# The last 11 taps of a 31-tap convolution on GpSimd instead of VectorE, in a two-block model kernel

## The chip, the cores and the metric

The kernel runs on one core of a Trainium2 chip. The metric is the device time of one execution in microseconds, as the median of several runs. The engines of the core that matter here are TensorE (matrix products; PE in the rows), VectorE (DVE), ScalarE (ACT) and GpSimd (POOL). Each works off its own queue in order and waits on semaphores for the others. SBUF is the memory on the chip that all of them read and write; products go to PSUM, which TensorE writes.

## What is computed

Two stacks of two layers over 256 tokens of width 1024. The change is in the mixer of the second stack, `hybrid_mixer`, which runs once in each of its two layers. It projects the normalised rows to several parts and feeds three branches: a gated linear attention (mLSTM, 4 heads), a gated convolution over 256 channels with 31 taps, and a softmax attention with decay (8 heads). Cut to the convolution:

```python
CONF_CHANNELS = D_MODEL // 4     # 256
CONF_KERNEL = 31

def causal_dwconv(x, w, b):
    K, C = w.shape
    y = lax.conv_general_dilated(
        x, w.astype(jnp.float32)[:, None, :], window_strides=(1,), padding=[(K - 1, 0)],
        dimension_numbers=("NWC", "WIO", "NWC"), feature_group_count=C)
    return y + b.astype(jnp.float32)

def hybrid_mixer(h, w_in, ...):
    z = jnp.einsum("bsd,de->bse", h, w_in).astype(jnp.float32)
    ...
    a, g = jnp.split(c_glu, 2, axis=-1)
    hc = causal_dwconv(a * jax.nn.sigmoid(g), conf_conv_w, conf_conv_b)
    hc = jax.nn.silu(layernorm_f32(hc, conf_ln_w, conf_ln_b))
    ...
    cat = jnp.concatenate([hm, hc, hf], axis=-1).astype(h.dtype)
    return jnp.einsum("bse,ed->bsd", cat, w_out)
```

So each of 256 channels is a sum over 31 shifts of its own row of 256 tokens, each times a number of that channel.

## The kernel before

The 256 channels lie as 2 halves of 128 partitions. `cf_in` holds the gated input, 2 x (30 + 256) columns with 30 zero columns ahead; `cf` is the accumulator, 128 x 2 x 256; `cw` and `cb` are weights and bias. `convolve` (line 2741) issues one VectorE instruction for each tap and half: for tap 0 a product with bias (line 2748, one input), for the others a product added to the accumulator (line 2749, both inputs in SBUF), 128x256 each. Each waits for the instruction two places ahead of it, which wrote the same half. `gate_glu` (line 2758) forms the gated input from two projection results, with one VectorE product of 128x512 (line 2760).

The list `glu` (line 2775) cuts this into nine steps: `glu[0]` the gate, `glu[1]` to `glu[7]` four taps each, `glu[8]` three. `hybrid_mixer` builds a list of jobs for `projection` (line 627), and puts `glu[0]` to `glu[4]` (16 taps) between the last projections. A job is one product on TensorE of a 128x2048 weight tile (48 matmuls of 128x256, since each product is made of three, line 129 to 131, over a high and a low part). The high part is rounded by ScalarE (line 112), the low part is what VectorE subtracts from it (line 116, 128x2048, both inputs in SBUF; called a split below). VectorE meets in its queue, from the gate on: taps 0 to 3, a split, taps 4 to 7, a split, taps 8 to 11, a split, taps 12 to 15. The three splits belong to the last three jobs (two give `h_fk`, the third `h_fv`). ScalarE takes their results (lines 2659, 2660), and between the last two it computes the exponentials of the decay and a sigmoid-weighted product (lines 2770 to 2773).

A join of all four engines ends the projection. Then come two calls of `attention` (line 674): first the softmax attention with 8 heads, 4 units of work, then the gated one with 4 heads, 2 units. VectorE's part is a loop over x: `prepare(x)` scales scores, `finish(x - 3)` normalises the output of a unit into `cat`, and `between[x]` runs what was handed in. Before, the first call runs `glu[5]` at x = 2 and `glu[6]` at x = 3, the second `glu[7]` at x = 2 and `glu[8]` at x = 3. At x = 1 of the second, VectorE also splits the first two weight tiles of the output projection. A join ends each call. `hybrid_tail` then transposes `cf` and `cat` on TensorE, normalises the convolution's channels and writes them to `cat[:, :, 256:512]`, whose columns nobody wrote before.

GpSimd in all this issues a few parameter transfers and three memsets, one of which clears the zero columns of `cf_in`, and then waits in the joins.

Of the kernel before, what the change touches and what calls it, by code (L numbers as in the profile page):

```python
# [12 lines left out]
ALU = mybir.AluOpType  # L13
# [3 lines left out]
P = 128  # L17
TOK = 256
# [2557 lines left out]
ML_H, ML_D, FX_H, FX_D = 4, 64, 8, 64  # L2576
ML_W, CF_W, FX_W = ML_H * ML_D, D // 4, FX_H * FX_D
ML_K, CF_K = 4, 31
# [69 lines left out]
def hybrid_mixer(c, layer, cat, buffers, claims, ahead):  # L2648

    nc, arg = c.nc, c.arg  # L2650
# [4 lines left out]
    def decay(buf, n, t):  # L2655
        return buf[:, 0:n * P].rearrange("p (h k) -> p h k", h=n) if t == 0 else \
            buf[:, n * P:].rearrange("p (h k) -> p h k", h=n)
# [5 lines left out]
    padded = c.sig("conv_padded")  # L2663
# [5 lines left out]
    step, convolved = c.sig("conv_step"), c.sig("convolved")  # L2669
# [71 lines left out]
    def convolve(dve, taps, n, x, acc, wt, b):  # L2741

        for k in taps:
            for i in range(n):
                if k:
                    dve.wait_ge(step.sem, step.count - n + 1)
                src = x[:, i, k:k + TOK]
                last = nc.vector.tensor_scalar(acc[:, i, :], src, wt[:, i, 0:1], b[:, i:i + 1], ALU.mult, ALU.add) if k == 0 else \
                    nc.vector.scalar_tensor_tensor(acc[:, i, :], src, wt[:, i, k:k + 1], acc[:, i, :], ALU.mult, ALU.add)  # L2749
                last.then_inc(*step.up())  # L2750

    def convolve_qk(dve):
# [2 lines left out]
        convolve(dve, range(ML_K), NT, qk_in, qk, mw, mb)  # L2755
        dve.drain().then_inc(*convolved.up())

    def gate_glu(dve):
        dve.wait_ge(*taken_act.at(4))
        c.dve(nc.vector.tensor_tensor(cf_in[:, :, cpad:], cf_in[:, :, cpad:], sg[:, :, :], ALU.mult))  # L2760

    def taps_glu(k0, k1):
        return lambda dve: convolve(dve, range(k0, k1), 2, cf_in, cf, cw, cb)

    def decay_exps(act):
# [6 lines left out]
        act.wait_ge(*convolved.at(1))  # L2772
        nc.scalar.activation(qk[:, :, :], qk[:, :, :], ACT.Silu)

    glu = [Step("dve", gate_glu)] + [Step("dve", taps_glu(k, min(k + 4, CF_K))) for k in range(0, CF_K, 4)]
    more = [
        Rows(c.xs, w, Z_V, HV, "act", cp(vo[:, :, 0:HV])),
        Cols(c.xs, w, Z_FQ, 256, "act", scaled_copy(fq[:, 0:2, :])),
# [22 lines left out]
    @c.block.gpsimd  # L2801
    def _(pool):
        pool.wait_ge(*c.sig("rms_turned").now())
# [4 lines left out]
    def _(pool):  # L2808
# [2 lines left out]
        nc.gpsimd.memset(fv[:, :, FX_W:], 0.0)  # L2811
        pool.drain().then_inc(*padded.up())
    projection(c, jobs, join=False)
    c.join()
    half = lambda i: slice((i % 2) * 64, (i % 2) * 64 + 64)
    third = c.xT[:, 0:2, :].rearrange("p k t -> p (k t)")
    attention(c, [(t, 0) for t in range(TT)], FX_H, FX_D,
# [1 line left out]
              v=lambda b, i, s: fv[:, s, i * FX_D:i * FX_D + P],  # L2819
              out=lambda t, b: cat[:, t, ML_W + CF_W:].rearrange("p (h d) -> p h d", h=FX_H),  # L2820
              scale=1.0, bias=lambda t, h, nk: decay(df, FX_H, t)[:, 4 * h:4 * h + 4],
              between={2: glu[5].run, 3: glu[6].run}, third=third)
    og = vo[:, :, ML_W:]

    @c.block.scalar
    def _(act):
# [2 lines left out]
              q=lambda t, b, i: qk[half(i), i // 2, t * P:(t + 1) * P], k=lambda b, i, nk: qk[half(i), 2 + i // 2, 0:nk],  # L2829
              v=lambda b, i, s: vo[:, s, i * ML_D:i * ML_D + P],  # L2830
              out=lambda t, b: cat[:, t, 0:ML_W].rearrange("p (h d) -> p h d", h=ML_H),
              scale=ML_D ** -0.5, bias=None, between={2: glu[7].run, 3: glu[8].run}, third=third,
              gated=(lambda t, nk: decay(dm, ML_H, t), lambda t: floor[:, t, :]))
    hybrid_tail(c, cat, cf, vo, norm_w, ln_w, ln_b)

# [290 lines left out]
def build(nc, arg, out):  # L3126
    with ExitStack() as ctx:
# [7 lines left out]
        def stages():  # L3135
# [21 lines left out]
            for layer in range(DEPTH):  # L3157
                with ExitStack() as m:
                    cat = c.sb(f"cat{2 + layer}", [P, TT, D], ctx=m)
                    gain = c.gain[:, :]  # L3160
                    if layer == 0:
                        gain = cat[:, 0, :]
                        load_ahead(c, "gain_landed", [(gain, bcast(arg["norm_mix_w_2"][0]))])
                        post_norm(c, columns=False)
                    hybrid_params = hybrid_buffers(c, layer, m)
                    pre_norm(c, gain)
                    jobs = residual_jobs(c, c.xs, arg["w_out_2"][layer], 1.0)
                    hybrid_mixer(c, layer, cat, hybrid_params, claims, lambda: claim(c, jobs))
                dense = []

                def claim_dense():
                    start, tiles = claim_dense_ffn(c)
                    dense.append(start)
                    return tiles
                cross_attention(c, layer, jobs, claim_dense if layer == 0 else None)
                if layer == 0:
                    claims = dense_ffn(c, dense[0])
                else:
                    flat_moe(c, layer)
# [42 lines left out]
```

## Time and profile before

| | us |
|---|---|
| median of 3 runs | 2651.18 |
| lowest and highest | 2651.12, 2653.88 |
| the profiled execution, time | 2649.35 |
| the profiled execution, span of the trace | 2647.6 |
| its mean granted TensorE clock, share of full speed | 0.939 |

Busy in the span: TensorE 2300.4 us (87%), VectorE 1798.0 (68%), ScalarE 1368.1 (52%), GpSimd 67.5 (3%). Times in the rows count from the start of the span. The 1.75 us that the profiled execution's time lies above its span stand around it and are not in the trace. A row's duration includes some overlap with the next: instructions of one engine that follow each other start a little before the one ahead ends.

### The profile page before, as it was taken

The page shows a single profiled execution, that of the slowest core. Times are in us where ns is not written, and L with a number is a line of the kernel's source. Part 1 is how long each engine was busy: PE and PEld are TensorE (multiplying, and loading weights), DVE is VectorE, ACT ScalarE, POOL GpSimd, SP SyncE. Part 2 cuts the span into 40 slices and gives each one's busy share as a digit, 9 for nine tenths or more (in the row PEclk, how much of TensorE's full clock was granted, in tenths as well). Part 3 has the DMA queues.
Part 4 walks back from the last instruction along what each step waited for, and adds up shares of the span by engine and source line. Part 5 has one row for each costly group of instructions (what it writes and reads, how often), then busy time and mean ns, then how long its engine had stood idle before and what let it go on. Part 6 is the DMA issues. An engine that isn't in the chain of part 4 may idle for free.

```text
span 2647.6 us, 43661 instructions
## 1 busy us (share of the span) xinstructions
PE 2300.4 (87%) x16404; PEld 2139.5 (81%) x16404; DVE 1798.0 (68%) x2101; ACT 1368.1 (52%) x1563; POOL 67.5 (3%) x111
## 2 busy tenths in 40 slices
PE   5568999788769999786889987777999999999997
PEld 4458999776569999775789877667999999998996
DVE  3457777434576765677456657646888888888886
ACT  3316556224345554444343344434777777777775
POOL 0010000000000000100000010000000000000000
PEclk8879999887889999898999999898999999999999
DMA  6227999460239998532345562333999999999993
GB/s 219 80 82 283 373 372 359 137 191 1 83 114 364 364 358 319 142 112 80 127 144 191 159 166 98 96 127 106 312 364 345 345 365 343 344 364 344 339 366 135
DMA packets 335529, 609.66 MB, mean 230 GB/s; under 512 B 11008, under 2 KB 266832, under 8 KB 310704
## 3 DMA queue, kind: packets, MB, share of 16 engines
q1 hardware_dynamic: 329696, 590.84, 63.9%
q0 software_dynamic: 5024, 13.16, 2.2%
q8 instruction: 185, 3.03, 0.5%
q10 hardware_dynamic: 560, 2.10, 0.2%
q14 instruction: 64, 0.52, 0.1%
HBM read 605.02 MB, written 1.05 MB: 229 GB/s over the span
## 4 chain that ended last, share of the span: by engine, by line
PE 77%; DVE 12%; ACT 4%; issue 3%; DVEq 2%; POOLq 1%; DMA 0%; ACTq 0%; POOL 0%; PEldq 0%
PE psum L129 16%; PE psum L131 16%; PE psum L130 16%; PE psum L1887 9%; PE psum L1923 9%; PE psum L1911 2%; DVE weight_ring_rounded L116 1%; PE psum L487 1%; DVE h_cf L2749 1%; ACT scores L760 1%; PE psum L2233 1%; PE psum L712 1%; PE psum L2420 1%; PE psum L548 1%; PE psum L309 1%
## 5 line engine op out<-in xcount | busy, mean ns | idle before, releaser
L1652 DVE TENSOR_TENSOR weight_ring_rounded<-weight_ring,weights_high_rounded 128x2048 fp32r<-128x2048 f32 x264 | 604.1, 2291 | 94.1 <-ACT weights_high_rounded L1647 93.9
L1647 ACT ACTIVATE weights_high_rounded<-weight_ring 128x2048 fp32r<-128x2048 f32 x264 | 504.7, 1915 | 105.4 <-PE psum L131 97.2
L129 PE MATMUL psum<-weights_high_rounded,scores_rounded 128*128 128x256 f32 x1408 | 406.2, 288 | 11.4 <-DVE scores_rounded L1684 10.5
L131 PE MATMUL psum<-weights_high_rounded,scores_rounded 128*128 128x256 f32 x1408 | 398.7, 283 | 0.0
L130 PE MATMUL psum<-weight_ring_rounded,scores_rounded 128*128 128x256 f32 x1408 | 398.4, 283 | 0.0
L1981 DVE TENSOR_TENSOR weight_ring_rounded<-weight_ring,weights_high_rounded 128x2048 fp32r<-128x2048 f32 x128 | 292.7, 2291 | 95.7 <-ACT weights_high_rounded L1976 95.7
L129 PEld LDWEIGHTS psum<-weights_high_rounded,scores_rounded 128*128 128x128 f32 x1408 | 270.0, 192 | 16.3 <-DVE scores_rounded L1684 12.1
L1887 PE MATMUL psum<-weights_high_rounded,scores_rounded 128*128 128x256 f32 x1024 | 263.7, 295 | 12.4 <-DVE scores_rounded L2060 10.7
L130 PEld LDWEIGHTS psum<-weight_ring_rounded,scores_rounded 128*128 128x128 f32 x1408 | 270.2, 192 | 3.4
L131 PEld LDWEIGHTS psum<-weights_high_rounded,scores_rounded 128*128 128x128 f32 x1408 | 270.0, 192 | 0.0
L131 PE MATMUL psum<-weights_high_rounded,xT_rounded 128*128 128x512 f32 (+3 forms) x688 | 261.5, 380 | 0.0
L1923 PE MATMUL psum<-xT_high,weight_ring 128*128 128x128 f32 x2048 | 241.6, 276 | 16.7 <-issue 12.3
L1887 PE MATMUL psum<-weight_ring_rounded,scores_rounded 128*128 128x256 f32 x1024 | 253.1, 285 | 0.0
L1923 PEld LDWEIGHTS psum<-xT_high,weight_ring 128*128 128x128 f32 x2048 | 234.6, 192 | 20.5 <-issue 15.8
L1976 ACT ACTIVATE weights_high_rounded<-weight_ring 128x2048 fp32r<-128x2048 f32 x128 | 243.7, 1905 | 3.2 <-POOLq L212 3.0
L129 PE MATMUL psum<-xT_high_rounded,weights_high_rounded 128*128 128x256 f32 x768 | 217.0, 283 | 14.8 <-DVE weight_ring_rounded L116 9.8
L116 DVE TENSOR_TENSOR weight_ring_rounded<-weight_ring,weights_high_rounded 128x2048 fp32r<-128x2048 f32 (+3 forms) x76 | 159.8, 2113 | 95.9 <-ACT weights_high_rounded L112 95.6
L131 PE MATMUL psum<-xT_high_rounded,weight_ring_rounded 128*128 128x256 f32 x768 | 215.5, 281 | 0.0
L1887 PEld LDWEIGHTS psum<-weights_high_rounded,scores_rounded 128*128 128x128 f32 x1024 | 197.7, 193 | 13.1 <-DVE scores_rounded L2060 10.9
L1887 PEld LDWEIGHTS psum<-weight_ring_rounded,scores_rounded 128*128 128x128 f32 x1024 | 198.2, 194 | 0.4 <-issue 0.4
L112 ACT ACTIVATE weights_high_rounded<-weight_ring 128x2048 fp32r<-128x2048 f32 (+3 forms) x76 | 133.8, 1768 | 117.4 <-PE psum L131 62.9
L130 PE MATMUL psum<-xT_rounded,weights_high_rounded 128*128 128x256 f32 x672 | 188.5, 281 | 0.0
(525 smaller groups left out, 4075.0 us busy)
## 6 DMA issues: line engine op xcount, KB each, us to landing
weight_ring<-in_moe_w_gate_dram SPq DMA_DIRECT2D x152, 1024.0 KB, 6.4
weight_ring<-in_moe_w_up_dram SPq DMA_DIRECT2D x152, 1024.0 KB, 8.4
weight_ring<-in_moe_w_down_dram SPq DMA_DIRECT2D x152, 1024.0 KB, 8.5
weight_ring<-in_w_in_dram SPq DMA_DIRECT2D x20, 1024.0 KB, 7.0
weight_ring<-in_ffn_w_gate_dram SPq DMA_DIRECT2D x11, 1024.0 KB, 5.4
weight_ring<-in_ffn_w_up_dram SPq DMA_DIRECT2D x11, 1024.0 KB, 5.3
weight_ring<-in_ffn_w_down_dram SPq DMA_DIRECT2D x11, 1024.0 KB, 4.9
weight_ring<-in_w_out_dram SPq DMA_DIRECT2D x8, 1024.0 KB, 5.0
```

What stands on the lines that cost most here:

```text
L112: self.ring.nc.scalar.activation(self.high, self.whole, ACT.Copy).then_inc(self.ring.high_ready, 1)
L116: self.ring.nc.vector.tensor_tensor(self.low, self.whole, self.high.bitcast(F32), ALU.subtract).then_inc(self.ring.split_ready, 1)
L129: nc.tensor.matmul(out, lh, rh, start=start, stop=False)
L130: nc.tensor.matmul(out, lh, rl, start=False, stop=False)
L131: return nc.tensor.matmul(out, ll, rh, start=False, stop=stop)
L1647: self.c.nc.scalar.activation(ring.high(self.s0 + q, 1, SLOT), ring.view(self.p0 + q, 1, SLOT), ACT.Copy).then_inc(ring.high_ready, 1)
L1652: self.c.nc.vector.tensor_tensor(ring.low(self.p0 + q, 1, SLOT), ring.view(self.p0 + q, 1, SLOT), ring.high(self.s0 + q, 1, SLOT).bitcast( ...
L1887: last = self.c.nc.tensor.matmul(psum[:, x % 2, a * CH:(a + 1) * CH], self.x[:, x % 2, k, :], w[:, k, :], start=(k == 0 and w is high), st ...
L1911: last = nc.tensor.matmul(psum[:, 2 + x % 2, at:at + self.W], blocks[:, a, m, :], self.twice, start=True, stop=True)
L1923: last = nc.tensor.matmul(psum[:, 4 + 2 * (x % 2) + k // 4, (k % 4) * P:(k % 4 + 1) * P], wt[:, m, k * P:(k + 1) * P], self.hidden[:, x % ...
L1976: self.c.nc.scalar.activation(ring.high(s, 1, SLOT), ring.view(self.gate_tile(x) + a, 1, SLOT), ACT.Copy).then_inc(ring.high_ready, 1)
L1981: self.c.nc.vector.tensor_tensor(ring.low(tile, 1, SLOT), ring.view(tile, 1, SLOT), ring.high(s, 1, SLOT).bitcast(F32), ALU.subtract).then ...
```

## The change

Taps 20 to 30 go to GpSimd. After the gate VectorE raises a signal, `gated`. GpSimd, once its three memsets are done, waits for it and then for each of the 11 taps multiplies both halves of the shifted input by the tap's weights, spread over the columns, in one instruction of 128x2x256; the first product goes to `late`, which is `cat[:, :, 256:512]`, each later one to `product`, `cat[:, :, 0:256]`, and is then added to `late` by a second instruction. That is 11 products and 10 sums, and each waits for the one ahead. The join at the end of the projection leaves GpSimd out. `glu` ends with `glu[5]`, which stays at x = 2 of the first attention; at x = 3 of it nothing is left. At x = 2 of the second attention VectorE waits for GpSimd's last signal and adds `late` to `cf`, one instruction of 128x512; at x = 3 nothing is left.

```diff
+    POOL_TAPS = 20
+    late, product = cat[:, :, ML_W:ML_W + CF_W], cat[:, :, 0:CF_W]
+    gated, pool_step, pool_conv = c.sig("glu_gated"), c.sig("pool_conv_step"), c.sig("pool_convolved")
+
     def gate_glu(dve):
         dve.wait_ge(*taken_act.at(4))
         c.dve(nc.vector.tensor_tensor(cf_in[:, :, cpad:], cf_in[:, :, cpad:], sg[:, :, :], ALU.mult))
+        dve.drain().then_inc(*gated.up())
+
+    def add_late(dve):
+        dve.wait_ge(step.sem, step.count)
+        dve.wait_ge(*pool_conv.now())
+        nc.vector.tensor_tensor(cf[:, :, :], cf[:, :, :], late, ALU.add)
...
-    glu = [Step("dve", gate_glu)] + [Step("dve", taps_glu(k, min(k + 4, CF_K))) for k in range(0, CF_K, 4)]
+    glu = [Step("dve", gate_glu)] + [Step("dve", taps_glu(k, min(k + 4, CF_K))) for k in range(0, POOL_TAPS, 4)]
...
     projection(c, jobs, join=False)
-    c.join()
+
+    @c.block.gpsimd
+    def _(pool):
+        pool.wait_ge(*padded.now())
+        pool.wait_ge(*gated.now())
+        for k in range(POOL_TAPS, CF_K):
+            x, w1 = cf_in[:, :, k:k + TOK], cw[:, :, k:k + 1].broadcast_to([P, 2, TOK])
+            if k == POOL_TAPS:
+                nc.gpsimd.tensor_tensor(late, x, w1, ALU.mult).then_inc(*pool_step.up())
+            else:
+                nc.gpsimd.tensor_tensor(product, x, w1, ALU.mult).then_inc(*pool_step.up())
+                pool.wait_ge(*pool_step.now())
+                nc.gpsimd.tensor_tensor(late, late, product, ALU.add).then_inc(*pool_step.up())
+                pool.wait_ge(*pool_step.now())
+        pool.drain().then_inc(*pool_conv.up())
+    c.join(pool=False)
...
-              between={2: glu[5].run, 3: glu[6].run}, third=third)
+              between={2: glu[5].run}, third=third)
...
-              scale=ML_D ** -0.5, bias=None, between={2: glu[7].run, 3: glu[8].run}, third=third,
+              scale=ML_D ** -0.5, bias=None, between={2: add_late}, third=third,
```

VectorE's queue at x = 1 to 3 of the second attention (`L116` the two splits, `L2749` tap steps, `L789` to `L806` the normalisations of the two units):

```order
 L116 TENSOR_TENSOR weight_ring_rounded<-weight_ring,weights_high_rounded 128x2048 [waits scores_scaled,high_parts_ready]
 L116 TENSOR_TENSOR weight_ring_rounded<-weight_ring,weights_high_rounded 128x2048 [waits high_parts_ready]
-L2749 SCALAR_TENSOR_TENSOR h_cf<-h_cf_in,h_cw,h_cf 128x256 [waits conv_step] x8
+L2770 TENSOR_TENSOR h_cf<-h_cf,cat 128x512 [waits pool_convolved,conv_step]
 L789 SCALAR_TENSOR_TENSOR row_sum<-row_sum 128x4 [waits pv_group_done]
 L790 TENSOR_TENSOR row_sum<-row_sum,h_floor 128x4 [waits dve_step]
 L793 RECIPROCAL recip<-row_sum 128x4 [waits dve_step]
 L806 TENSOR_TENSOR cat<-psum,recip 128x256 [waits dve_step]
-L2749 SCALAR_TENSOR_TENSOR h_cf<-h_cf_in,h_cw,h_cf 128x256 [waits conv_step] x6
```

The eight tap steps ahead of the first normalisation became one addition that waits for GpSimd, and the six between the two normalisations went.

GpSimd's queue behind its memsets, in the first of the two layers (the last two rows shown repeat nine times more):

```order
+L2825 UNCONDITIONAL_BRANCH
+L2832 TENSOR_TENSOR cat2<-h0_cf_in,h0_cw 128x2x256 [waits glu_gated,conv_padded]
+L2834 TENSOR_TENSOR cat2<-h0_cf_in,h0_cw 128x2x256
+L2836 TENSOR_TENSOR cat2<-cat2 128x2x256 [waits pool_conv_step]
+L2834 TENSOR_TENSOR cat2<-h0_cf_in,h0_cw 128x2x256 [waits pool_conv_step]
+L2836 TENSOR_TENSOR cat2<-cat2 128x2x256 [waits pool_conv_step]
```

Where GpSimd went on to the join, it now has 21 instructions. VectorE's queue inside the projection, gate, taps 0 to 15 and three splits, is the same before and after, but for the signal behind the gate:

```order
L2760 TENSOR_TENSOR h_cf_in<-h_cf_in,scores 128x2x256 [waits results_taken_act]
L2748 TENSOR_SCALAR h_cf<-h_cf_in,h_cw,h_cb 128x256 [waits dve_step]
L2748 TENSOR_SCALAR h_cf<-h_cf_in,h_cw,h_cb 128x256
L2749 SCALAR_TENSOR_TENSOR h_cf<-h_cf_in,h_cw,h_cf 128x256 [waits conv_step] x6
L116 TENSOR_TENSOR weight_ring_rounded<-weight_ring,weights_high_rounded 128x2048 [waits high_parts_ready]
L2749 SCALAR_TENSOR_TENSOR h_cf<-h_cf_in,h_cw,h_cf 128x256 [waits conv_step] x8
```

These six rows are those of before; a split and eight tap steps follow twice more.

## Rows read from the trace of the kernel before

**Rows 1.** The page: chain that ended last, by engine.
```profile
PE 77%; DVE 12%; ACT 4%; issue 3%; DVEq 2%; POOLq 1%; DMA 0%; ACTq 0%; POOL 0%; PEldq 0%
```

**Rows 2.** Busy time by stretch: end of projection, two attentions, first layer, then second.
```profile
core 0: us, PE busy (x) PEld busy (x) DVE busy (x) ACT busy (x) POOL busy (x), PEclk, DMA share, GB/s
1144.60:1171.00 26.40, 18.92 (x150) 18.56 (x148) 19.21 (x35) 10.72 (x18) 0.00 (x0) 0.94 0.42 132
1171.00:1192.10 21.10, 14.86 (x104) 11.90 (x104) 14.14 (x44) 11.76 (x40) 0.00 (x0) 0.84 0.09 36
1192.10:1208.20 16.10, 6.29 (x53) 5.21 (x53) 14.45 (x34) 7.00 (x8) 0.00 (x0) 0.88 0.00 1
1602.00:1628.40 26.40, 19.11 (x151) 18.74 (x150) 19.19 (x35) 10.75 (x18) 0.00 (x0) 0.94 0.42 132
```

**Rows 3.** Timeline of VectorE, projection: start, duration, instruction, count.
```profile
1143.88 0.69 DVE L2760 TENSOR_TENSOR h_cf_in<-h_cf_in,scores 128x512 f32<-128x512 f32 x1
1144.60 0.73 DVE L2748 TENSOR_SCALAR h_cf<-h_cf_in,h_cw,h_cb 128x256 f32<-128x256 f32 x2
1145.25 2.46 DVE L2749 SCALAR_TENSOR_TENSOR h_cf<-h_cf_in,h_cw,h_cf 128x256 f32<-128x256 f32 x6
1147.63 2.28 DVE L116 TENSOR_TENSOR weight_ring_rounded<-weight_ring,weights_high_rounded 128x2048 fp32r<-128x2048 f32 x1
...
1158.37 2.28 DVE L116 TENSOR_TENSOR weight_ring_rounded<-weight_ring,weights_high_rounded 128x2048 fp32r<-128x2048 f32 x1
1160.57 3.24 DVE L2749 SCALAR_TENSOR_TENSOR h_cf<-h_cf_in,h_cw,h_cf 128x256 f32<-128x256 f32 x8
```

**Rows 4.** Timeline of TensorE: last three jobs, start of attention; idle before in brackets.
```profile
1150.06 0.55 PE L129 MATMUL psum<-xT_high_rounded,weights_high_rounded 128*128 128x256 f32 x1 [4.87 <-DVE weight_ring_rounded L116]
...
1157.13 0.28 PE L129 MATMUL psum<-xT_high_rounded,weights_high_rounded 128*128 128x256 f32 x1
...
1162.78 0.28 PE L129 MATMUL psum<-weights_high_rounded,xT_high_rounded 128*128 128x256 f32 x1
...
1168.12 0.28 PE L131 MATMUL psum<-weights_high_rounded,xT_rounded 128*128 128x256 f32 x1
1171.00 1.16 PE L712 MATMUL psum<-h_fk,h_fq 64*128 64x128 f32 x16 [2.61 <-POOLq L212]
```

**Rows 5.** Timeline of ScalarE, end of projection.
```profile
1170.13 0.58 ACT L2659 ACTIVATE h_fv<-psum 128x512 f32<-128x512 f32 x1
```

**Rows 6.** Chain of waits through both attentions: start, duration, what.
```profile
1185.27 3.16 DVE h_cf L2749 x8
...
1200.45 3.17 DVE h_cf L2749 x8
...
1204.56 2.37 DVE h_cf L2749 x6
```

**Rows 7.** Timeline of TensorE, behind the tap steps of the first attention.
```profile
1189.12 1.13 PE L735 MATMUL psum<-h_fv,probs_turned 128*128 128x128 f32 x8 [0.39 <-DVE cat L806]
```

**Rows 8.** Timeline of GpSimd at two routings, first stack and last layer.
```profile
172.98 2.40 POOL L2174 CAST e_outT<-e_outT 128x512 f32<-128x512 int32 x1
175.33 1.80 POOL L2175 MEMSET e_xg<- 128x2048 f32 x1
...
1795.20 0.55 POOL L2173 IOTA f_outT<- 128x512 int32 x1 [11.19 <-DVEq L206]
1795.82 0.61 POOL L2174 CAST f_outT<-f_outT 128x512 f32<-128x512 int32 x1
```

**Rows 9.** Timeline of VectorE beside them.
```profile
172.62 2.29 DVE L2118 TENSOR_TENSOR weights_high_rounded<-x,weights_high_rounded 128x2048 fp32r<-128x2048 f32 x1 [1.49 <-ACT weights_high_rounded L2113]
...
176.04 1.11 DVE L2511 CAST r_idx_g<-r_firsti 128x2 f32<-128x2 uint32 x1
...
1797.38 2.29 DVE L2118 TENSOR_TENSOR weights_high_rounded<-f_outT,weights_high_rounded 128x2048 fp32r<-128x2048 f32 x1 [1.59 <-ACT weights_high_rounded L2113]
```

**Rows 10.** Groups of VectorE by form: busy, mean ns of one.
```profile
L2524 DVE CAST r_idx<-r_topi 128x4 f32<-128x4 uint32 x2 | 0.3, 170 | 0.1
```

## The prediction

> **What bounds the kernel now.** I read the page's chain first, then the busy times by stretch, then the chain of waits through the hybrid mixer, the only place the change touches. Over the whole span TensorE holds 77% of the chain and VectorE 12% [rows 1]. The convolution lies in one of the few stretches where VectorE is the limit. The mixer runs twice, once per layer, with the same pattern 457 us apart [rows 2]. In the stretch from the gated product to the end of the projection VectorE is busy 19.2 of 26.4 us, in the two attentions 14.1 of 21.1 and 14.4 of 16.1 us; GpSimd is empty in all of them.
>
> Inside the projection stretch [rows 3], VectorE runs without a gap from 1144.6 to 1163.8: two first-tap products, 6 tap steps, a weight split, 8 tap steps, a split, 8, a split, 8. A tap step costs 0.41 us by spacing (3.24 us for 8), a split 2.2 to 2.3 us. TensorE has already waited 4.87 us for the first of these splits, takes 7.1 us for the job behind that wait (1150.06 to 1157.13) and 5.65 for the next, of as many matmuls, which it starts without one (to 1162.78). Its first matmul after the wait lasts 0.55 us, the later ones 0.28: the lower and the higher of the clock's two levels, 1.2 and 2.4 GHz. It issues its last matmul at 1168.12 [rows 4]. The third split, ready at 1158.37 + 2.28 = 1160.65, thus has 2.1 us of slack before TensorE needs it. The last result leaves ScalarE at 1170.71, because the exponentials stand ahead of it there [rows 5]; this ends the projection, and attention starts at 1171.0.
>
> In the attentions the chain [rows 6] goes through the tap steps directly: 3.16 us late in the first attention, and 3.17 and 2.37 us in the second.
>
> **What leaves VectorE.** Per layer 22 tap steps go, in groups of 8 (first attention), 8 and 6 (second); the 8 steps of the first attention's earlier place stay. First attention: the 3.16 us stand in the chain, but TensorE had then waited only 0.39 us for the result behind them [rows 7]; next late are the copies on ScalarE. I take 0.4 us. Second attention: VectorE goes from the two weight splits straight through taps and normalisations to the end, so 3.17 + 2.37 = 5.5 us come off in full. One addition of 128x512 is added, priced by the gating product of the same shape, 0.69 us [rows 3]. Gain there 4.8 us, 5.2 us per layer, 10.4 us in all. What is next late there is the tail's own chain, unchanged.
>
> The signal behind the gating product costs a drain that VectorE had in effect paid (it waited for that product anyway): zero. The join that GpSimd no longer takes part in is put down to GpSimd's queue in TensorE's row [rows 4], but GpSimd had nothing to do there; ScalarE came last, at 1170.71, so leaving GpSimd out gives nothing. GpSimd's next transfers (the memory rows and the next parameters) are issued after the later joins, as before; the queue is only moved past by 21 instructions that must be over by the end of the mixer.
>
> **What GpSimd adds.** 21 two-input products and sums per layer, 11 and 10, each 128x512, each waiting for the one before. The trace has no two-input operation on GpSimd. The nearest is a cast of the same shape with one input, 0.61 us, and the next instruction behind a wait on its own signal starts 0.07 us after the end (1795.20 + 0.55 to 1795.82) [rows 8]. Lower bound 0.61 us, if a second operand is free; upper bound 1.8 us, three times that. I take twice the cast, 1.2 us, since two operands are read for each result. The 21 then need 21 x 1.27 = 26.7 us, against about 56 us from 1144.9 until the addition that consumes them is due (some 1200). So by itself the work fits and nobody waits for it.
>
> The Trainium skill (GPSIMD Engine Reference, section Elementwise — side-by-side cycle accounting) gives 4497 ns for a two-input fp32 operation of 2048 elements per partition. Scaled to 512 that is an estimate of 1.12 us, and with it the sum below would end near 2683. No row here shows such an operation.
>
> **What it costs VectorE.** This is the term that decides. The trace shows GpSimd and VectorE shutting each other out. The cast that takes 0.61 us alone took 2.40 us when it started at 172.98, 0.36 us behind a VectorE subtraction with two SBUF inputs: it ended at 175.38, 0.47 us after that instruction had ended at 174.91 [rows 8, 9]. It did not run at part speed beside it, it stood. In the other direction a VectorE cast of 2 elements per partition took 1.11 us, from 176.04 to 177.15, where its sibling takes 0.17 [rows 9, 10]; GpSimd's memset beside it ended at 177.13 [rows 8]. The same subtraction begun at 1797.38 under a GpSimd memset kept its 2.29 us [rows 9], so an operation that only writes does not disturb it. The tap steps, and the splits too, are two-input operations in SBUF like that subtraction, and all 21 GpSimd operations read SBUF.
>
> What no row shows is a two-input VectorE instruction that comes behind a reading GpSimd one. The Trainium skill (SBUF — State Buffer, section Who interferes with whom) says that such a pair contends for a shared read interface and that whoever starts first holds it for the whole instruction, whichever engine that is. The trace agrees in the direction it shows.
>
> I take it that the two alternate: each GpSimd operation, ready 0.07 us after its predecessor, finds a VectorE step of 0.4 us running, waits for its end, then runs for 1.2 us while the next VectorE step stands. Counting two-input VectorE instructions up to and including the third split gives 6 + 1 + 8 + 1 + 8 + 1 = 25, enough to interleave all 21. The first overlaps the one-input first taps by 0.4 us. So the third split ends 21 x 1.2 - 0.4 = 24.8 us later, at 1185.4. TensorE starts its last job 0.2 us later and, coming out of a wait at half clock, needs 7.1 us for it (as from 1150.06 to 1157.13 [rows 4]); the copy takes 0.6. The projection ends at 1193.3 instead of 1170.7, **+22.6 us**. Slack of 2.1 us and the 2.3 us between TensorE's and ScalarE's ends are used up in this; the exponentials on ScalarE, moved along, stay hidden under the last job.
>
> Per layer: +22.6 - 5.2 = +17.4 us; twice +34.8. Against the profiled execution's 2649.35 this is 2684; the median shown is 1.8 us above it (0.07%), so I predict **2685 us**. Nothing returns it later: in both mixers TensorE is idle for the whole delay.
>
> **The rivals.**
> 1. *VectorE keeps the turn, or loses nothing.* If steps issued back to back leave no opening, or such a pair does not collide, GpSimd works only in VectorE's pauses: 8 us before attention (1163.8 to 1171.8) and those of the attentions. From 1145 to 1200.4 that is 55.4 us less 18.8 in the projection, 3.2 of taps and 4.4 of splits, 29 us for 26.7 of work. Cost to VectorE 0 to 2.4 us a layer, so 10.4 us minus at most 4.8: **2641 to 2646**. For it: back-to-back steps overlap in the trace (0.475 us long, 0.41 apart). Against it: the blocked cast of 2 elements shows that GpSimd's hold is respected too.
> 2. *One GpSimd operation for every two VectorE ones.* Then 12 fall before the third split: 14.4 - 0.4 = 14.0 us; TensorE ends at 1181.9, copy 1182.5, +11.8; the other 9 lie in VectorE's pause and cost nothing. 2 x (11.8 - 5.2) = +13: **2664**.
> 3. *The operation is at an end of its bounds.* At 0.61 us the third split is 12.4 us late, +10.2 at the end of the projection, 2 x 5.0: **2661**. At 1.8 us it is 37.4 us late, +35.2, 2 x 30.0: **2711**.
> 4. *GpSimd is late, not VectorE.* If VectorE keeps the turn and an operation takes 1.5 us, 21 of them need 33.0 us of the 29 that VectorE leaves free; the addition, which stands on VectorE ahead of both normalisations of the second attention, waits 4.1 us, and TensorE's tail waits for those. Of the 4.8 + 0.4 us gained 1 is left: no change, **about 2650**. The waiting begins at an operation of 1.3 us; from 1.6 us on it is a loss (at 1.8 us 39.3 us, 10 late, 2661).
>
> **How the numbers follow.** Alternation with an operation of 1.0 to 1.4 us: 50%, 2677 to 2694. Rival 2: 15%. Rival 3: 6% short, 9% long. Rival 1: 13%. Rival 4: 7%. Rival 1 alone is faster by over 0.2% (5.3 us, about what a measurement of this kernel can tell from no change): 0.14 with a little of rival 4. Same 0.07, slower 0.79. The range runs from rival 4 to between 2694 and the long end, **2650 to 2704**, leaving out rival 1 and most of the long case.
>
> **What would show it.** In the trace after: GpSimd operations at 1.2 us alone, longer beside VectorE; tap steps in the projection of about 1.6 us spacing instead of 0.41, splits of 3.4 instead of 2.3; TensorE waiting for the second and third split, where it now waits only for the first; a projection stretch of about 49 us instead of 26.4, and a second attention near 11.3 instead of 16.1. It is wrong if tap steps keep their 0.41 us while GpSimd is busy (rival 1), if they come in pairs between long ones (rival 2), or if the addition is preceded by an idle VectorE (rival 4).

## The result

The changed kernel takes 2678.84 us (median of 4, 2677.98 to 2681.14) against 2652.53 us; the ratio is 1.0095, 95% interval 1.0075 to 1.0115. It is slower, by some 25 us. Predicted was 2685 us, 6 us more; as a change that was 34 us, so the loss was forecast a third too large.

Where it went shows best from three marks in each mixer: the gating product on VectorE, the first score matmul of the first attention, that of the second, and the first transpose of the tail.

| us, first layer / second layer | before | after | difference |
|---|---|---|---|
| gate to first attention | 27.12 / 27.12 | 44.31 / 44.19 | +17.2 / +17.1 |
| first attention | 21.12 / 21.12 | 20.51 / 20.65 | -0.6 / -0.5 |
| second attention | 16.07 / 16.07 | 11.13 / 11.13 | -4.9 / -4.9 |

That is +11.7 us a layer, 23.3 in all, inside the interval of the ratio (19.9 to 30.5 us). The two profiled executions differ by more, 31.8 us of span. 7.5 us of this have arisen before the first mixer's gate (1143.88 before, 1151.42 after), in code that the change leaves alone; in the nine experiments this mark lies between 1147.5 and 1160.2 us, without relation to the edits. So comparisons below count from the gate, and totals are taken from the ratios.

Busy time of the kernel after by the same three stretches (columns as in [rows 2]; the first starts at the end of the gate):

```profile
core 0: us, PE busy (x) PEld busy (x) DVE busy (x) ACT busy (x) POOL busy (x), PEclk, DMA share, GB/s
1152.14:1195.73 43.59, 22.99 (x151) 22.45 (x149) 38.20 (x35) 10.74 (x18) 29.01 (x21) 0.77 0.24 77
1195.73:1216.24 20.51, 14.76 (x104) 11.95 (x104) 11.08 (x36) 11.81 (x40) 0.00 (x0) 0.83 0.11 42
1216.24:1227.37 11.13, 6.28 (x52) 5.19 (x52) 9.52 (x21) 6.97 (x8) 0.00 (x0) 1.00 0.01 1
```

VectorE still has 35 instructions in the first stretch, but they last 38.2 us instead of 19.2. All 21 GpSimd operations lie in it. VectorE's timeline there, which answers [rows 3]:

```profile
1152.27 2.30 DVE L2748 TENSOR_SCALAR h_cf<-h_cf_in,h_cw,h_cb 128x256 f32<-128x256 f32 x2
1154.49 7.89 DVE L2749 SCALAR_TENSOR_TENSOR h_cf<-h_cf_in,h_cw,h_cf 128x256 f32<-128x256 f32 x6
1162.31 3.34 DVE L116 TENSOR_TENSOR weight_ring_rounded<-weight_ring,weights_high_rounded 128x2048 fp32r<-128x2048 f32 x1
1165.57 10.48 DVE L2749 SCALAR_TENSOR_TENSOR h_cf<-h_cf_in,h_cw,h_cf 128x256 f32<-128x256 f32 x8
1175.98 3.13 DVE L116 TENSOR_TENSOR weight_ring_rounded<-weight_ring,weights_high_rounded 128x2048 fp32r<-128x2048 f32 x1
1179.03 6.07 DVE L2749 SCALAR_TENSOR_TENSOR h_cf<-h_cf_in,h_cw,h_cf 128x256 f32<-128x256 f32 x8
1185.02 2.29 DVE L116 TENSOR_TENSOR weight_ring_rounded<-weight_ring,weights_high_rounded 128x2048 fp32r<-128x2048 f32 x1
```

Tap steps stand 1.3 us apart instead of 0.41 (7.89 for 6, 10.48 for 8), until GpSimd is done at 1182.84; the last split takes its old 2.29. GpSimd's timeline beside it:

```profile
1152.33 1.04 POOL L2832 TENSOR_TENSOR cat<-h_cf_in,h_cw 128x512 f32<-128x512 f32 x1 [55.66 <-DVEq L2765]
1153.34 1.08 POOL L2834 TENSOR_TENSOR cat<-h_cf_in,h_cw 128x512 f32<-128x512 f32 x1
...
1162.18 1.32 POOL L2836 TENSOR_TENSOR cat<-cat 128x512 f32<-128x512 f32 x1
1163.58 2.97 POOL L2834 TENSOR_TENSOR cat<-h_cf_in,h_cw 128x512 f32<-128x512 f32 x1
1166.63 1.34 POOL L2836 TENSOR_TENSOR cat<-cat 128x512 f32<-128x512 f32 x1
...
1177.04 3.20 POOL L2836 TENSOR_TENSOR cat<-cat 128x512 f32<-128x512 f32 x1
...
1181.50 1.34 POOL L2836 TENSOR_TENSOR cat<-cat 128x512 f32<-128x512 f32 x1
```

A product takes 1.04 to 1.10 us, a sum 1.26 to 1.36, except for the two that met a split: 2.97 and 3.20. The two engines need not touch the same data for this: the sum at 1162.18 reads and writes `cat`, the split at 1162.31 reads weights and takes 3.34 us instead of 2.28. TensorE's timeline, with what ended its waits, which answers [rows 4]:

```profile
1165.80 0.55 PE L129 MATMUL psum<-xT_high_rounded,weights_high_rounded 128*128 128x256 f32 x1 [13.06 <-DVE weight_ring_rounded L116]
...
1179.25 0.55 PE L129 MATMUL psum<-xT_high_rounded,weights_high_rounded 128*128 128x256 f32 x1 [5.15 <-DVE weight_ring_rounded L116]
...
1195.73 1.05 PE L712 MATMUL psum<-h_fk,h_fq 64*128 64x128 f32 x14 [2.38 <-ACTq L201]
```

It waited 4.87 us for splits in this stretch before, now 18.2 in two waits. The third split, for which the prediction had it wait too, was ready just in time: at 1187.31, and the last job started at 1187.49 without a wait. In the second attention the addition stands where the taps stood and waits for nobody:

```profile
1220.09 4.49 DVE L116 TENSOR_TENSOR weight_ring_rounded<-weight_ring,weights_high_rounded 128x2048 fp32r<-128x2048 f32 x2 [0.29 <-ACT weights_high_rounded L112]
1224.49 0.69 DVE L2770 TENSOR_TENSOR h_cf<-h_cf,cat 128x512 f32<-128x512 f32 x1
```

### The profile page after: what moved, and what is told of

Same layout as the page of the kernel before. It is cut to its first block, busy times and chain, and to the rows that moved or that the text cites. A ratio compares the mean times of both kernels' runs of the same rounds, so it can differ in the third digit from the quotient of the medians.

```text
span 2679.4 us, 43665 instructions
## 1 busy us (share of the span) xinstructions
PE 2310.9 (86%) x16404; PEld 2148.2 (80%) x16404; DVE 1819.4 (68%) x2059; ACT 1369.8 (51%) x1563; POOL 125.8 (5%) x153
## 4 chain that ended last, share of the span: by engine, by line
PE 76%; DVE 12%; ACT 4%; issue 4%; DVEq 2%; POOLq 1%; DMA 0%; ACTq 0%; POOL 0%; PEldq 0%
PE psum L129 15%; PE psum L131 15%; PE psum L130 15%; PE psum L1887 9%; PE psum L1923 9%; PE psum L1911 2%; DVE h_cf L2749 2%; DVE weight_ring_rounded L116 2%; PE psum L487 1%; ACT scores L760 1%; PE psum L2233 1%; PE psum L735 1%; PE psum L712 1%; PE psum L2420 1%; PE psum L309 1%
## 5 line engine op out<-in xcount | busy, mean ns | idle before, releaser
L116 DVE TENSOR_TENSOR weight_ring_rounded<-weight_ring,weights_high_rounded 128x2048 fp32r<-128x2048 f32 (+3 forms) x76 | 163.7, 2164 | 97.3 <-ACT weights_high_rounded L112 96.8
```

Source lines behind the costliest of these rows:

```text
L116: self.ring.nc.vector.tensor_tensor(self.low, self.whole, self.high.bitcast(F32), ALU.subtract).then_inc(self.ring.split_ready, 1)
```

## Is it GpSimd's work, and nothing else of the change?

Theory: VectorE and GpSimd take turns, so that a VectorE instruction stands while a GpSimd operation reads. Rival: the signal, the drain or the join without GpSimd slows the projection. Two kernels take one half of the change each. `left_out`:

```diff
-        nc.vector.tensor_tensor(cf[:, :, :], cf[:, :, :], late, ALU.add)
...
-        for k in range(POOL_TAPS, CF_K):
-            x, w1 = cf_in[:, :, k:k + TOK], cw[:, :, k:k + 1].broadcast_to([P, 2, TOK])
-            if k == POOL_TAPS:
-                nc.gpsimd.tensor_tensor(late, x, w1, ALU.mult).then_inc(*pool_step.up())
-            else:
-                nc.gpsimd.tensor_tensor(product, x, w1, ALU.mult).then_inc(*pool_step.up())
...
-              scale=ML_D ** -0.5, bias=None, between={2: add_late}, third=third,
+              scale=ML_D ** -0.5, bias=None, between={}, third=third,
```

> The changed kernel with GpSimd's 21 operations and the added sum taken out: the last 11 taps are not computed at all; the signal behind the gate and the join without GpSimd stay. Theory of turns (VectorE stands while a GpSimd operation reads): the whole loss lies in GpSimd's operations, so tap steps are back at 0.41 us, the stretch from the gate to attention is 27.1 us as before, and the two attentions are 6.5 us a layer shorter, 5.8 as measured after plus 0.69 for the sum: 2652.5 - 13 = 2639.5, ratio 0.995. Rival, the loss comes from the signal, the drain or the join: the stretch stays near 44 us and the time near 2675.

`both`:

```diff
-        nc.vector.tensor_tensor(cf[:, :, :], cf[:, :, :], late, ALU.add)
+        glu[7].run(dve)
...
-    glu = [Step("dve", gate_glu)] + [Step("dve", taps_glu(k, min(k + 4, CF_K))) for k in range(0, POOL_TAPS, 4)]
+    glu = [Step("dve", gate_glu)] + [Step("dve", taps_glu(k, min(k + 4, CF_K))) for k in range(0, CF_K, 4)]
...
-              between={2: glu[5].run}, third=third)
+              between={2: glu[5].run, 3: glu[6].run}, third=third)
...
-              scale=ML_D ** -0.5, bias=None, between={2: add_late}, third=third,
+              scale=ML_D ** -0.5, bias=None, between={2: add_late, 3: glu[8].run}, third=third,
```

> GpSimd's 21 operations of the changed kernel beside all 31 taps on VectorE as before; GpSimd's sum is computed and thrown away, and no tap is missing. Theory of turns: the stretch from the gate to attention is 44.3 us as in the changed kernel (27.1 before), the attentions as before, 2652.5 + 2 x 17.2 = 2687, ratio 1.013. Rival, the two engines do not disturb each other and the change loses by its order or a wait: ratio 1.000.

| | ratio to before | gate to first attention | first attention | second |
|---|---|---|---|---|
| left_out | 0.9951 (0.9934 to 0.9968) | 27.4 / 27.2 | 20.5 / 20.6 | 10.5 / 10.5 |
| both | 1.0125 (1.0100 to 1.0150) | 44.2 / 44.1 | 21.1 / 21.1 | 16.1 / 16.1 |
| after | 1.0095 (1.0075 to 1.0115) | 44.3 / 44.2 | 20.5 / 20.7 | 11.1 / 11.1 |

The two halves fit together without a rest: the whole loss of the stretch comes with GpSimd's operations, the whole gain with the taps taken from VectorE, and signal and join cost 0.1 to 0.3 us (27.4 and 27.2 against 27.12). The rival is out. First stretch of `both`:

```profile
1155.25:1198.75 43.50, 22.73 (x150) 22.16 (x149) 38.20 (x35) 10.72 (x18) 29.02 (x21) 0.76 0.25 80
```

## What of GpSimd collides: reading, writing, or being busy?

`memsets` puts in the place of each operation a memset of about its length, which reads nothing; the last 11 taps are thus left out. It was run once:

```diff
-                nc.gpsimd.tensor_tensor(product, x, w1, ALU.mult).then_inc(*pool_step.up())
+                nc.gpsimd.memset(cat[:, :, 0:ML_W + CF_W], 0.0).then_inc(*pool_step.up())
```

(and so for the first product and the sums).

> The changed kernel with each of GpSimd's 21 operations replaced by a memset of 1024 elements a partition, about as long (0.95 us from the memset of 960 in the trace), at the same place in its queue and with the same waits; the last 11 taps are not computed, and the zeros are added. Theory that what collides is GpSimd's reading: the tap steps of two inputs go back to 0.41 us and splits to 2.3 while GpSimd is busy, and the stretch from the gate to attention is 27 to 29 us. The two first-tap instructions (one input) took 1.1 us each beside GpSimd's products; if they keep that beside memsets, it is GpSimd's writing that stops them. Rival, any busy GpSimd stops VectorE: tap steps of 1.0 to 1.3 us and a stretch of about 42 us.

VectorE, then GpSimd, in this kernel:

```profile
1148.36 2.17 DVE L2748 TENSOR_SCALAR h_cf<-h_cf_in,h_cw,h_cb 128x256 f32<-128x256 f32 x2
1150.44 2.45 DVE L2749 SCALAR_TENSOR_TENSOR h_cf<-h_cf_in,h_cw,h_cf 128x256 f32<-128x256 f32 x6
1152.81 2.28 DVE L116 TENSOR_TENSOR weight_ring_rounded<-weight_ring,weights_high_rounded 128x2048 fp32r<-128x2048 f32 x1
```

```profile
1150.44 0.98 POOL L2837 MEMSET cat<- 128x1024 f32 x1
1151.47 0.95 POOL L2835 MEMSET cat<- 128x1024 f32 x1
1152.48 0.95 POOL L2837 MEMSET cat<- 128x1024 f32 x1
```

Tap steps (2.45 us for 6) and splits (2.28) have their old times while GpSimd is 94% busy. The two first-tap instructions, of one input, stay at 1.1 us each, where they take 0.73 together otherwise. The stretch is 29.7 and 29.5 us: of its 2.4 to 2.6 us more, 1.5 are these two instructions and the signal: the first split is ready that much later. The rest is TensorE's clock: after the longer wait 24 and 22 of its matmuls stand 0.21 us apart (the lower level) instead of 13, and each of these costs 0.1 us more than one at the higher level. So a two-input VectorE instruction collides with a GpSimd operation that reads and not with one that only writes, and a one-input TENSOR_SCALAR with both. Why the second kind collides the traces suggest: in the kernel before, 128x1024 of it take 0.744 us (line 3004) and 128x256 take 0.410, 0.43 ns an element, where a two-input instruction of 128x2048 and one of 128x512 differ by 1.04 ns an element (2.28 and 0.69 us). By these times it moves about two elements where the other moves one. The Trainium skill (VectorE: DVE Perf Modes, section Mode 2×_2P — use both read ports for one tensor) says that such single-input instructions use both read and both write ports; the memset run agrees.

## Turns, or the time that GpSimd is busy?

`halves` cuts each operation into two of 128x256, 42 in all:

```diff
-                nc.gpsimd.tensor_tensor(product, x, w1, ALU.mult).then_inc(*pool_step.up())
-                pool.wait_ge(*pool_step.now())
-                nc.gpsimd.tensor_tensor(late, late, product, ALU.add).then_inc(*pool_step.up())
-                pool.wait_ge(*pool_step.now())
+                for i in range(2):
+                    nc.gpsimd.tensor_tensor(product[:, i], x[:, i], w1[:, i], ALU.mult).then_inc(*pool_step.up())
+                    pool.wait_ge(*pool_step.now())
+                for i in range(2):
+                    nc.gpsimd.tensor_tensor(late[:, i], late[:, i], product[:, i], ALU.add).then_inc(*pool_step.up())
+                    pool.wait_ge(*pool_step.now())
```

> The changed kernel with each GpSimd operation cut into two of 128x256, 42 in all; nothing else differs. Theory of strict turns: one GpSimd operation fits between two VectorE ones whatever its length, so the tap step beside it falls from 1.3 to about 0.75 us; 27 VectorE instructions up to the third split lose about 0.33 us each, the stretch is near 36 us instead of 44.3, and GpSimd runs on into VectorE's pause. Rival, VectorE loses the time that GpSimd is busy, however cut: the stretch stays at 44 us or more and tap steps at 1.3 us on average.

VectorE in this kernel:

```profile
1151.82 4.81 DVE L2749 SCALAR_TENSOR_TENSOR h_cf<-h_cf_in,h_cw,h_cf 128x256 f32<-128x256 f32 x6
1156.55 2.81 DVE L116 TENSOR_TENSOR weight_ring_rounded<-weight_ring,weights_high_rounded 128x2048 fp32r<-128x2048 f32 x1
1159.28 6.58 DVE L2749 SCALAR_TENSOR_TENSOR h_cf<-h_cf_in,h_cw,h_cf 128x256 f32<-128x256 f32 x8
```

Tap steps stand 0.81 us apart, and the stretch is 35.1 and 37.7 us instead of 44.3, though GpSimd does the same sums with more overhead and works until 1189, into the first attention. The expectation was 36. The layers differ by the clock: the last job has one matmul at TensorE's lower level in the first layer and 27 in the second. So VectorE's loss goes by the period of GpSimd's operations, to which each of its short instructions is stretched, and not by GpSimd's busy time. The kernel was run once, in 2660.4 us against 2657.2 for before in the same job; the stretches, with the attentions, ask for 6.6 more. That one time settles nothing, the stretches carry the argument.

`five_taps` leaves only 9 GpSimd operations:

```diff
-    POOL_TAPS = 20
+    POOL_TAPS = 26
...
+    def glu_seven(dve):
+        glu[7].run(dve)
+        add_late(dve)
...
-              between={2: glu[5].run}, third=third)
+              between={2: glu[5].run, 3: glu[6].run}, third=third)
...
-              scale=ML_D ** -0.5, bias=None, between={2: add_late}, third=third,
+              scale=ML_D ** -0.5, bias=None, between={2: glu_seven}, third=third,
```

> The changed kernel with only the last 5 taps on GpSimd (9 operations), the other 26 on VectorE at their former places. Theory of turns: 9 operations stand in front of the first split only; it ends 8 us late, the later two meet a free VectorE, and TensorE, which waits for the first, takes the whole of it: stretch 35 us instead of 27.1. The second attention keeps 4 of 14 tap steps and the sum, 3.2 us shorter. Net +5 a layer: 2656 + 10, ratio 1.004. Rival, the cost is in proportion to the operations (9 of 21): stretch 34.5 us, which is as good as the same; rival, few operations fit into slack: stretch below 30 us and ratio 0.998.

The kernel did not do quite what this says: its last group ran to tap 27, so taps 26 and 27 were added on VectorE too. `five_taps_once` mends that:

```diff
-    glu = [Step("dve", gate_glu)] + [Step("dve", taps_glu(k, min(k + 4, CF_K))) for k in range(0, POOL_TAPS, 4)]
+    glu = [Step("dve", gate_glu)] + [Step("dve", taps_glu(k, min(k + 4, POOL_TAPS))) for k in range(0, POOL_TAPS, 4)]
```

> The last 5 taps on GpSimd (9 operations) and 26 taps on VectorE, each tap once: in the kernel five_taps VectorE also computed taps 26 and 27, 4 tap steps more in the second attention than meant. Theory of turns: the stretch from the gate to attention stays at 35.3 us, the second attention goes from 14.4 to 12.8 us. Net a layer +8.2 - 3.2 = +5, ratio 1.004 with 1.002 to 1.006 allowed. Rival, the 4 steps more were hidden: second attention 14.4 us.

The stretches are 35.3 and 36.0 us with the slip, 36.2 and 36.0 mended; the second attention 14.4 and 12.8 us. Ratios 1.0066 (1.0042 to 1.0089) and 1.0057 (1.0039 to 1.0075), the second near the top of what was allowed. VectorE, mended:

```profile
1155.15 7.90 DVE L2749 SCALAR_TENSOR_TENSOR h_cf<-h_cf_in,h_cw,h_cf 128x256 f32<-128x256 f32 x6
1162.97 3.35 DVE L116 TENSOR_TENSOR weight_ring_rounded<-weight_ring,weights_high_rounded 128x2048 fp32r<-128x2048 f32 x1
1166.24 3.24 DVE L2749 SCALAR_TENSOR_TENSOR h_cf<-h_cf_in,h_cw,h_cf 128x256 f32<-128x256 f32 x8
1169.41 2.28 DVE L116 TENSOR_TENSOR weight_ring_rounded<-weight_ring,weights_high_rounded 128x2048 fp32r<-128x2048 f32 x1
```

All nine are done or under way when the first split starts, the one for which TensorE waits anyway (13.08 us here, 4.87 before), and after them VectorE has its old times. Five taps cost 9 us there: the split comes 8.2 us later, 0.9 for each operation, and the rest is TensorE at its lower level for 10 matmuls more. They bring 3.2 us in the second attention. A few operations at the place without slack cost their full turn.

## Is it the work, or its place?

`late_start` gives GpSimd the same 11 taps but starts it when VectorE is done with the projection:

```diff
+    def free(dve):
+        dve.drain().then_inc(*vector_free.up())
...
-        glu[:2] + more[1:2] + glu[2:3] + more[2:3] + glu[3:4] + more[3:4] + glu[4:5] + more[4:])
+        glu[:2] + more[1:2] + glu[2:3] + more[2:3] + glu[3:4] + more[3:4] + glu[4:5] + more[4:] + [Step("dve", free)])
...
         pool.wait_ge(*gated.now())
+        pool.wait_ge(*vector_free.now())
```

> The changed kernel, but GpSimd waits until VectorE has finished its part of the projection (the 16 taps and three splits). Theory of turns: the stretch from the gate to attention is back at 27.1 us; GpSimd's 21 operations (27 us) run from 1164 on this clock, beside VectorE's pause and the first attention; the 8 tap steps there stand for 0.9 us each, about 7 us a layer, and the end of GpSimd's work at about 1193 is before the sum at about 1198. Net a layer -5.8 + 7 = +1, ratio between 0.998 and 1.003. Rival, the two do not disturb each other: 2652.5 - 11.6 = 2641, ratio 0.9956. Rival, GpSimd then ends too late: VectorE idle before the sum.

The ratio is 1.0029 (1.0019 to 1.0039). The stretch is back at 27.4 us, the first attention takes 29.8 instead of 21.1, the second 11.1. VectorE in the first attention:

```profile
1194.63 0.42 DVE L831 CUSTOM_DVE_ANT_0 scores<-psum,h_df 128x256 f32<-128x256 f32 x1 [3.59 <-PE psum L712]
...
1196.33 10.42 DVE L2749 SCALAR_TENSOR_TENSOR h_cf<-h_cf_in,h_cw,h_cf 128x256 f32<-128x256 f32 x8 [0.23 <-issue]
```

The 8 tap steps take 10.42 us instead of 3.26, 7.2 more, as expected (7). The scaling of scores keeps its 0.42 us with GpSimd busy: one of its inputs comes from PSUM. GpSimd's operations beside such instructions:

```profile
1192.45 1.26 POOL L2841 TENSOR_TENSOR cat<-cat 128x512 f32<-128x512 f32 x1
1193.80 1.04 POOL L2839 TENSOR_TENSOR cat<-h_cf_in,h_cw 128x512 f32<-128x512 f32 x1
1194.92 1.27 POOL L2841 TENSOR_TENSOR cat<-cat 128x512 f32<-128x512 f32 x1
1196.27 1.04 POOL L2839 TENSOR_TENSOR cat<-h_cf_in,h_cw 128x512 f32<-128x512 f32 x1
1197.38 1.33 POOL L2841 TENSOR_TENSOR cat<-cat 128x512 f32<-128x512 f32 x1
```

Both of the engines' times are undisturbed until the tap steps start at 1196.33; then a GpSimd pair goes from 2.47 us (1193.80 to 1196.27) to 2.58, and each tap step loses 0.9. TensorE waits for what comes behind them:

```profile
1209.44 1.11 PE L721 MATMUL psum<-ident,scores 128*128 128x128 f32 x4 [8.98 <-ACT scores L760]
```

The first attention is 9.3 us longer than in the changed kernel, 2.1 more than the tap steps. These 2.1 us lie behind this wait: from there to the second attention it takes 7.88 us (1209.44 to 1217.32), against 5.78 in the changed kernel behind a wait of 1.81, and the granted clock of the attention is 0.71 instead of 0.83. The expectation of 1 us a layer left this out; by the marks it is 4.

If the place decides, the taps need not leave VectorE. `moved` is the kernel before with its last 15 taps at its idle times, 8 us ahead of the first attention and 3.6 us behind its second unit:

```diff
-        glu[:2] + more[1:2] + glu[2:3] + more[2:3] + glu[3:4] + more[3:4] + glu[4:5] + more[4:])
+        glu[:2] + more[1:2] + glu[2:3] + more[2:3] + glu[3:4] + more[3:4] + glu[4:5] + more[4:] + glu[5:7])
...
-              between={2: glu[5].run, 3: glu[6].run}, third=third)
+              between={1: glu[7].run, 3: glu[8].run}, third=third)
...
-              scale=ML_D ** -0.5, bias=None, between={2: glu[7].run, 3: glu[8].run}, third=third,
+              scale=ML_D ** -0.5, bias=None, between={}, third=third,
```

> The kernel before, without GpSimd, with VectorE's last 15 taps at other places: taps 16 to 23 at the end of the projection, where VectorE is idle for 8 us, taps 24 to 27 at x = 1 of the first attention, ahead of an idle time of 3.6 us, taps 28 to 30 at x = 3 of it, none in the second. If what the taps cost is their place and not their number, 2.9 us of the first attention and 5.5 us of the second go, a layer: 2652.5 - 17 = 2635.5, ratio 0.9936. Rival: the pauses are needed (weights, clock) and the time stays.

0.9949 (0.9931 to 0.9968), 2644.43 us against 2656.11 in the same job: faster than both kernels. VectorE:

```profile
1170.51 9.59 DVE L2749 SCALAR_TENSOR_TENSOR h_cf<-h_cf_in,h_cw,h_cf 128x256 f32<-128x256 f32 x24
1181.77 0.69 DVE L840 SCALAR_TENSOR_TENSOR scores<-psum,h_df 128x512 f32<-128x512 f32 x1 [1.68 <-PE psum L712]
...
1184.41 3.25 DVE L2749 SCALAR_TENSOR_TENSOR h_cf<-h_cf_in,h_cw,h_cf 128x256 f32<-128x256 f32 x8
1188.09 0.42 DVE L831 CUSTOM_DVE_ANT_0 scores<-psum,h_df 128x256 f32<-128x256 f32 x1 [0.42 <-PE psum L712]
```

24 tap steps in a row fill the time ahead of the attention and leave 1.68 us of it; 8 more fill the pause behind the second unit and leave 0.42 us. The three stretches are 27.2, 18.6 and 10.5 us, in all 8.0 us less in the first layer (7.1 in the second). The ratio gives 13.5 us (8 to 18), the expectation was 17.

`mixed` is the same idea with GpSimd at a place where nothing collides: taps 16 to 23 on VectorE at the end of the projection, the last 7 on GpSimd from then on, and their addition at the end of the first attention:

```diff
-    POOL_TAPS = 20
+    POOL_TAPS = 24
...
-        glu[:2] + more[1:2] + glu[2:3] + more[2:3] + glu[3:4] + more[3:4] + glu[4:5] + more[4:])
+        glu[:2] + more[1:2] + glu[2:3] + more[2:3] + glu[3:4] + more[3:4] + glu[4:5] + more[4:] + glu[5:7] + [Step("dve", free)])
...
+        pool.wait_ge(*vector_free.now())
...
-              between={2: glu[5].run}, third=third)
+              between={6: add_late}, third=third)
...
-              scale=ML_D ** -0.5, bias=None, between={2: add_late}, third=third,
+              scale=ML_D ** -0.5, bias=None, between={}, third=third,
```

> Taps 16 to 23 on VectorE at the end of the projection, the last 7 taps on GpSimd (13 operations, 16 us), started only then, beside the first attention, in which VectorE now has no tap steps; the sum at its end; no tap step in the second attention. Theory of turns: VectorE's attention instructions read one operand from PSUM and kept their times beside GpSimd before, so nothing collides; the first attention is about 18.5 us (18.6 with the taps moved on VectorE alone), the second 10.5: ratio 0.994 to 0.995, no better than the moved taps without GpSimd. Rival, GpSimd ends after the first attention: VectorE idle before the sum, ratio nearer 0.997.

0.9948 (0.9930 to 0.9966), the same as without GpSimd. Its stretches are 27.3, 19.2 and 10.5 us. GpSimd is done at 1192.15, and the addition stands at 1195.30 for 0.68 us. The first attention is 0.6 us longer than in `moved` in the first layer and as long in the second (19.1). So GpSimd can do this work without harm, but VectorE's idle time was enough for it.

## Why the prediction was right, and where it was off

- **What leaves VectorE.** Predicted 5.2 us a layer, 0.4 in the first attention and 4.8 in the second; measured 0.5 to 0.6 and 4.9. `left_out` has 5.5 in the second, the 5.5 of the two tap groups without the addition.
- **GpSimd's operation.** Taken at 1.2 us between bounds of 0.61 and 1.8. Measured 1.04 to 1.10 for a product, 1.26 to 1.36 for a sum, some 1.2 on the mean; the gap between two is 0.07 to 0.08 us, as read from [rows 8]. The Trainium skill's figure (GPSIMD Engine Reference, section Elementwise — side-by-side cycle accounting), by the estimate 1.12 us, is also near.
- **The turns.** The order was as forecast, one operation for each VectorE instruction: 21 operations fall beside the two first taps and the next two tap groups and splits, and three steps of the third. The size was off. The step that failed is "then runs for 1.2 us while the next VectorE step stands": I added GpSimd's whole 1.2 us to the tap's 0.4, a period of 1.67 us. Measured is 1.29, GpSimd's own period (1.18 for a product, 1.40 for a sum) and hardly more than its 1.24 alone, so most of the tap step must fit into GpSimd's gap and start; it costs GpSimd 0.05 us. VectorE loses 0.9 us a turn, not 1.2. A split of 2.2 us does not fit; there both lose.
- **The first taps.** I took the two one-input instructions to be free of it; they took 2.30 us instead of 0.73. The trace of before could have told, by their time an element. These 1.6 us worked against the turns that were taken too long.
- **The sum.** The third split came 19.1 us late instead of 24.8. And it was not the one that decided: the second, ready 27.7 us behind the gate instead of 11.4, started TensorE's last job but one at 1179.25. That one took 8.2 us, longer than the 7.1 I took for a job behind a wait, since after waits of 13.06 and 5.15 us TensorE stayed at the lower clock level for about 26 matmuls (0.21 us apart until 1184.9; granted clock of the stretch 0.77, before 0.94). In the 7.1 us of before it was some 13, and not only the first one behind the wait, as my reading had it. ScalarE's work behind its result, 7.8 us with the exponentials, then ended the projection: +17.2 us instead of +22.6. In my sum it lay hidden under the last job. Its first and last instruction:

```profile
1187.69 0.60 ACT L2659 ACTIVATE h_fk<-psum 128x512 f32<-128x512 f32 x1 [12.95 <-PE psum L131]
...
1194.86 0.58 ACT L2659 ACTIVATE h_fv<-psum 128x512 f32<-128x512 f32 x1
```

- **The whole.** +11.7 us a layer instead of +17.4, nearly all of the difference in the projection's term. That my path through the third split, with its measured 19.1 us, would have given +16.9, near the +17.2, is luck: the path ran through the second split and ScalarE. Also, 2649.35, 34.8 and 1.8 add up to 2686, not 2685. Rivals 1 and 4 (VectorE keeps the turn) are refuted by the 1.3 us spacing, rival 2 (every other turn) by the one-to-one count, rival 3 by the operation's own time, and nobody waited for GpSimd.

## What to carry to other kernels

Two-input elementwise work given to GpSimd is not beside VectorE if VectorE's own instructions then read two operands from SBUF: here each short one was stretched to GpSimd's period, from 0.41 to 1.3 us. That GpSimd was hardly used before (3% of the span) does not help. What matters is which instructions VectorE runs in that time and whether TensorE waits for them. Those with an operand in PSUM kept their times here (0.42 and 0.69 us in `late_start`), and GpSimd memsets touched only the fast one-input ones. A long wait of TensorE costs more than itself, since it works at the lower clock level behind it: 1.2 us in the changed kernel's last job but one, 2.1 us in `late_start`. Before moving work to another engine, look for the idle times of its own: here 15 taps moved within VectorE's queue gave half a per cent, the same as the best use of GpSimd that was tried.

## What the runs showed of the hardware beyond what was expected

- The turn costs the GpSimd operation almost nothing when the VectorE instruction is short (a pair of operations 2.58 us instead of 2.47 with 0.41 us tap steps between), and VectorE all of it. Beside a 2.2 us split GpSimd's operation takes 2.97 to 3.20 us.
- A one-input fp32 TENSOR_SCALAR between SBUF tensors, 0.32 to 0.37 us a piece, is stopped by GpSimd memsets too (1.1 us a piece); two-input instructions are not.
- A GpSimd sum of two computed tensors takes 1.27 us against 1.04 for a product whose second operand is one number spread over the columns, both 128x512 and undisturbed. Whether the operation or the operand makes the difference was not tried.
